# A two-block transformer kernel: earlier first matmuls, paired stick-breaking values, and another order of weight splits, taps and head copies

## The chip, the cores and the metric

One core of a Trainium2 chip. The metric is the device time of one execution in microseconds (us), the median of several runs. Matrix products run on TensorE (PE), elementwise work on VectorE (DVE), ScalarE (ACT) and GpSimd (POOL); SyncE (SP) issues most of the loads.

## What is computed

Two blocks over 512 positions of width 1024, in float32:

```python
# first block
h = rmsnorm(x, attn_norm_w); proj = h @ w_in              # 24 tiles of 128 columns
y_sb = stick_breaking_attention(q_a, k_a, v_a)            # 4 heads of 64
y_ch = chunked_relpos_attention(qh, kh, v_b, rel_bias)    # 8 heads
y_cv = short_conv_mixer(g_b, g_c, x_c, conv_w)
x = x + group_rmsnorm(concat(y_sb, y_ch, y_cv)) @ w_out
x = x + swiglu(rmsnorm(x), w_gate, w_up, w_down)
# second block
proj = rmsnorm_2(x) @ w_in_2 + b_in_2                     # 42 tiles of 128 columns
conv = silu(layernorm(causal depthwise conv, 31 taps, of val * sigmoid(gate))) @ w_conv_out
attn = sliding-window attention with sinks (16 heads, 2 kv heads, rope) @ w_attn_o
x = x + gated sum of both @ w_out_2
x = x + peer(rmsnorm_2(x))                                # 16384 experts, top 16
```

The stick-breaking weights of a head are `exp(log_sigmoid(z) + sum of log(1-beta) over nearer keys)`, and the output is these weights times v.

## The kernel before

**Layout and weights.** Activations are kept transposed: 128 channels of a tile on the partitions, the 512 positions along the free axis. Every large product is made of three fp32r matmuls per 128x128 piece of weights (`three`, L1094 to L1098): high weights times high input, high times low, low times high. So each weight slot (128x2048 elements, two output tiles of eight pieces, or k steps) is loaded into `raw`, ACT makes the rounded high part `wh` (`high`, L562 to L566) and DVE or POOL the rest `wl = raw - wh` (`weight_low`, L1708 to L1711). There are two buffers of each: ACT may write `wh` of a slot when PE has finished the slot two before it (`w_used`), PE may start a slot when its `wl` is there (`w_lo`). Inside a slot, columns 256k to 256k+255 belong to step k, 128 for each of its two output tiles. Each engine runs its own list, written out by hand, and waits on semaphores.

**The start.** SP loads x in four pairs of tiles and slot 0 in two parts, columns 0 to 511 and 512 to 2047 (L405 to L412); ACT's queue loads `vec` (all per-channel vectors, 389 columns) and later `cst`. ACT makes the high parts of x and of slot 0 (`x_high`, L569 to L572; `first_high`, L615 to L618), DVE the low ones (`x_low`, `first_low`, L1714 to L1717). PE takes the first two tiles interleaved, k step by k step (L1171 to L1177), waiting for slot 0's second part at k = 2, then tiles 2 and 3 out of slot 1, tiles 4 and 5 out of slot 2.

**Stick-breaking heads** (L1238 to L1272). For each of four heads n, PE computes four score products (`sb_scores`, L1219), nine chunks of the projection as cover (a chunk is one k step of a tile, three matmuls), the reverse sums (`sb_sums`, L1226 to L1234), five more chunks, and the values product (`sb_values`, L1238 to L1250). The scores' logs are made by ACT in the buffer `ab` (`sb_logs`, L682 to L698), softplus and masks by DVE (L1748 to L1777). All heads use one `ab`, so `sb_logs(n)` waits for the values of head n-1 (`sb_pv`). The values product has four matmuls of 512, 384, 256 and 128 columns with 64 output rows: an even head fills partitions 0 to 63 of bank 4, an odd one 64 to 127. The chunked heads that follow have a values product too (L1310), in which the matmuls of two heads alternate.

**The second block's projection** (PE L1443 to L1484, ACT L893 to L926, DVE L2080 to L2110). 42 tiles in 21 slots, g0 = FIRST["in2"], slots g0 to g0+20. Tiles 0 to 5 run on unscaled x, whose scaled high and low parts are made meanwhile (`scaled_x`, `scaled_high`); later tiles use the scaled ones. ACT evicts tile t-1 in step t (`in2_out`) and makes the high part of the slot two ahead in odd steps. DVE does the 31-tap convolution, two channel tiles alternating, one product and 31 taps each, 256 operations in all, handed out in numbers by `taps(count)`, and `weight_low`. In DVE's step t the order is: beats, `scaled_out`, for even t up to 6 `weight_low(g0+t/2+1)`, ropes, taps (5 in even, 7 in odd steps from 6 to 21), and for even t from 8 on `weight_low(g0+t/2+1)`. From tile 22 on the sliding-window attention runs between the pieces in 35 beats:

```python
def beat_place(n):
    chunk = n * (Z2_TILES - BEAT_TILE0) * KD // BEATS   # 42, 22, 8, 35
    return BEAT_TILE0 + chunk // KD, chunk % KD
```

so beats 0 to 5 stand before pieces (22,0), (22,4), (23,1), (23,5), (24,2), (24,6). PE's beat n is scores(n) (L1388), the transposes of beat n-2 (L1399), and the values of beat n-3 (L1412). scores(n) waits for DVE's `masked(n-1)` (L2065, semaphore `sw_m`), scores(0) for the first rope (`sw_q`). DVE's beat n: one tap, `masked(n)`, one tap, a rope of the next head pair if n % 4 = 1 (with one tap), two taps. ACT's beat n: for n = 7, 11, ... first `heads_out` (two copies, L863 and L869), then `turned_weights(n-2)` (L856), on which PE's values wait, then the exponentials and scales of beat n (L835 to L847).

**What the change touches:** L239 to L240 (buffers), L405 to L412, L560, L613 to L634, L688 to L710, L871 to L878, L911 to L917, L1171 to L1181, L1238 to L1272, L1666, L1714 to L1727, L1755, L1776, L2091 to L2106.

Of the kernel before, what the change touches and what calls it, by code (L numbers as in the profile page):

```python
# [15 lines left out]
P = 128  # L16
# [163 lines left out]
def build(nc, ins, out):  # L180
    with ExitStack() as ctx:
# [57 lines left out]

        csc = (z1[:, 0:2, :], z1[:, 2:4, :], ab[:, 0:2, :])  # L240
# [154 lines left out]
        def _(sp):  # L395
# [163 lines left out]
        def _(act):  # L559
            act.dma_start(vec[:, :], ins["vec"]).then_inc(sem("vec_in"), 16)  # L560
# [52 lines left out]
            act.wait_ge(sem("vec_in"), 16)  # L613

            def first_high(sem_in, part):  # L615
                c = slice(512 * part, 512 if part == 0 else 2048)
                act.wait_ge(sem(sem_in), 16)
                act.activation(wh[:, 0, c], raw[:, 0, c], ACT.Copy).then_inc(sem("w_hi" if part else "w0_hi"), 1)  # L618

            for k in range(KD):  # L620
                if k % 2 == 0:
                    act.wait_ge(sem(f"x_in{k // 2}"), 16)
                x_high(0, k)
                if k == 0:
                    first_high("w0_raw", 0)
                if k == 2:
                    first_high("w_raw0", 1)
                    act.dma_start(cst[:, :, :], ins["cst"]).then_inc(sem("cst_in"), 16)
            high(1, 1)
            for k in range(KD):  # L630
                x_square(0, k)
            high(2, 0)
            norm(0, 2)
# [48 lines left out]
            def sb_logs(n):  # L682

                for a in range(NT + 2):
                    if a < NT:
                        b, w, i = NT - 1 - a, (a + 1) * P, 4 * n + a + 1
                        act.wait_ge(sem("sb_z"), i)
                        if n:  # L688
                            act.wait_ge(sem("sb_pv"), n)
                        act.activation(ab[:, b, 0:w], ps[:, b, 0:w], ACT.Abs).then_inc(sem("sb_abs"), 1)  # L690
                    if 0 <= a - 1 < NT:
                        b, w, i = NT - a, a * P, 4 * n + a
                        act.wait_ge(sem("sb_abs"), i)
                        act.activation(ab[:, b, 0:w], ab[:, b, 0:w], ACT.Exp, scale=-1.0).then_inc(sem("sb_e"), 1)
                    if a >= 2:
                        b, w, i = NT + 1 - a, (a - 1) * P, 4 * n + a - 1
                        act.wait_ge(sem("sb_e"), i)
                        act.activation(ab[:, b, 0:w], ab[:, b, 0:w], ACT.Ln, bias=v("one")).then_inc(sem("sb_l"), 1)  # L698

            def sb_weights(n):  # L700

                for a in range(NT):
                    b, w, i = NT - 1 - a, (a + 1) * P, 4 * n + a + 1
                    act.wait_ge(sem("sb_cum"), i)
                    act.activation(ab[:, b, 0:w], ps[:, b, 0:w], ACT.Exp).then_inc(sem("sb_w0"), 1)

            def sb_out(p):

                act.wait_ge(sem("sb_pv"), 2 * p + 2)
# [191 lines left out]
            for t in range(Z2_TILES + 1):  # L901
# [9 lines left out]
                if t >= 4:  # L911
                    in2_out(t - 1)
# [1537 lines left out]
```

## Time and profile before

| | us |
|---|---|
| Runs before (3): median, lowest, highest | 2642.7, 2642.53, 2644.01 |
| The profiled execution's own time | 2642.51 |
| Its span, first to last instruction | 2640.7 |
| PE busy | 2609.4 (99%) |
| DVE busy | 1606.1 (61%) |
| ACT busy | 1042.4 (39%) |
| POOL busy | 432.6 (16%) |

The execution's time is 1.8 us more than its span. A busy PE is a PE with a matmul under way; matmul rows give start and length, and a steady stream overlaps, so its pace is read from starts. "Idle before <- X" names what ended an engine's idle time. The rows of an engine are read in order of time; L numbers are lines of the kernel before.

### The profile page before, as it was taken

To read this page: it belongs to the slowest core of one execution; us is meant where nothing else is said; L and a number is where in the kernel's file an instruction comes from. 1 tells how busy PE (TensorE), PEld (TensorE's weight loads), DVE (VectorE), ACT (ScalarE), POOL (GpSimd) and SP (SyncE) were. 2 spreads that over 40 slices of the span, in tenths; PEclk is the share of its full clock that TensorE was granted. 3 is DMA by queue.
4 is the path that set the end of the run, shared out by engine and by line. 5 is a ranking of instruction groups with operands and counts; after the bars stand their busy time and mean duration, and the time that the engine had idled before them with its cause. 6 is when DMAs were issued, how large, how long until landed. Compare 5 with 4: busy or idle time off the path is not lost.

```text
span 2640.7 us, 33826 instructions
## 1 busy us (share of the span) xinstructions
PE 2609.4 (99%) x12608; PEld 2115.0 (80%) x12608; DVE 1606.1 (61%) x2402; ACT 1042.4 (39%) x1349; POOL 432.6 (16%) x179
## 2 busy tenths in 40 slices
PE   8999999999999999999999999999999999999998
PEld 6777888888776788888888888888888888888886
DVE  4577211203999976579998988888344444444444
ACT  4565322214347763232223555555322222222223
POOL 0001455542021104434444000000000000000000
PEclk9999999999999999999999999999999999999999
DMA  5112222222222222224333454464565555555552
GB/s 185 48 51 78 96 95 95 100 96 96 96 84 76 69 96 96 106 77 145 146 147 142 171 212 183 191 238 183 214 216 192 194 195 195 195 193 195 195 191 96
DMA packets 121736, 374.37 MB, mean 142 GB/s; under 512 B 7552, under 2 KB 73216, under 8 KB 92736
## 3 DMA queue, kind: packets, MB, share of 16 engines
q1 hardware_dynamic: 117968, 333.74, 35.8%
q10 hardware_dynamic: 2016, 35.26, 3.4%
q0 software_dynamic: 1680, 4.46, 0.6%
q8 instruction: 39, 0.64, 0.1%
q14 instruction: 33, 0.27, 0.0%
HBM read 301.86 MB, written 69.21 MB: 141 GB/s over the span
## 4 chain that ended last, share of the span: by engine, by line
PE 92%; DVE 6%; ACT 1%; issue 1%; DMA 0%; POOL 0%; POOLq 0%; SPq 0%; DVEq 0%; ACTq 0%
PE ps L1096 28%; PE ps L1098 28%; PE ps L1097 28%; DVE z L2004 3%; PE ps L1619 2%; DVE wl L1711 1%; PE ps L1577 0%; PE ps L1399 0%; PE ps L1283 0%; ACT wh L566 0%; PE ps L1294 0%; PE ps L1412 0%; PE ps L1388 0%; PE ps L1310 0%; PE ps L1219 0%
## 5 line engine op out<-in xcount | busy, mean ns | idle before, releaser
L1096 PE MATMUL ps<-hh,wh 128*128 128x512 f32 x1968 | 783.9, 398 | 10.8 <-DVE wl L1717 8.5
L1098 PE MATMUL ps<-hh,wl 128*128 128x512 f32 x1968 | 769.0, 391 | 0.0
L1097 PE MATMUL ps<-hl,wh 128*128 128x512 f32 x1968 | 768.1, 390 | 0.0
L566 ACT ACTIVATE wh<-raw 128x2048 fp32r<-128x2048 f32 x217 | 414.8, 1912 | 774.3 <-PE ps L1098 772.5
L2293 DVE TENSOR_TENSOR wl<-raw,wh 128x2048 fp32r<-128x2048 f32 x101 | 231.3, 2290 | 432.1 <-ACT wh L566 432.1
L1096 PEld LDWEIGHTS ps<-hh,wh 128*128 128x128 f32 x1968 | 370.4, 188 | 101.2 <-issue 15.3
L1098 PEld LDWEIGHTS ps<-hh,wl 128*128 128x128 f32 x1968 | 370.3, 188 | 79.1
L1097 PEld LDWEIGHTS ps<-hl,wh 128*128 128x128 f32 x1968 | 370.9, 188 | 74.1 <-issue 0.7
L1097 PE MATMUL ps<-gal,wh 128*128 128x512 f32 x1024 | 398.7, 389 | 0.0
L1096 PE MATMUL ps<-gah,wh 128*128 128x512 f32 x1024 | 398.7, 389 | 0.0
L1098 PE MATMUL ps<-gah,wl 128*128 128x512 f32 x1024 | 398.7, 389 | 0.0
L478 POOL TENSOR_TENSOR wl<-raw,wh 128x2048 fp32r<-128x2048 f32 x50 | 230.4, 4608 | 588.4 <-ACT wh L566 588.4
L1097 PEld LDWEIGHTS ps<-gal,wh 128*128 128x128 f32 x1024 | 192.3, 188 | 39.8
L1096 PEld LDWEIGHTS ps<-gah,wh 128*128 128x128 f32 x1024 | 192.3, 188 | 39.8
L1098 PEld LDWEIGHTS ps<-gah,wl 128*128 128x128 f32 x1024 | 192.3, 188 | 39.8
L555 POOL TENSOR_TENSOR pf<-pf,at 128x512 f32<-128x512 f32 x3 | 3.7, 1265 | 1183.6 <-ACT at L1083 1183.6
L2004 DVE SCALAR_TENSOR_TENSOR z<-z,vec 128x511 f32<-128x511 f32 (+14 forms) x240 | 161.0, 731 | 0.0
L547 POOL TENSOR_TENSOR wl<-raw,wh 128x2048 fp32r<-128x2048 f32 x27 | 128.0, 4740 | 183.6 <-ACT wh L566 183.6
L1000 ACT ACTIVATE ast<-ps 128x512 f32<-128x512 f32 x64 | 38.2, 598 | 240.9 <-PE ps L1098 240.9
L1045 ACT ACTIVATE stage<-ps 128x512 f32<-128x512 f32 x128 | 129.4, 1122 | 0.0
L1035 ACT ACTIVATE ast<-ps 128x512 f32<-128x512 f32 x64 | 38.2, 597 | 194.8 <-PE ps L1098 194.8
L2307 DVE TENSOR_TENSOR same<-iota_t,slot_t 128x1024 f16<-128x1024 f16 x64 | 79.2, 1237 | 43.8 <-PE ps L1619 37.9
(289 smaller groups left out, 3038.6 us busy)
## 6 DMA issues: line engine op xcount, KB each, us to landing
raw<-in_w_slots SPq DMA_DIRECT2D x217, 1024.0 KB, 4.8
a_spill<-ast SPq DMA_DIRECT2D x64, 512.0 KB, 2.6
gate_table<-stage ACTq DMA_DIRECT2D x8, 4096.0 KB, 13.0
at<-a_spill SPq DMA_DIRECT2D x64, 512.0 KB, 5.7
tt<-gate_table SPq DMA_DIRECT2D x64, 512.0 KB, 6.8
lnb<-z POOLq DMA_DIRECT2D x36, 64.0 KB, 2.0
xT<-in_x SPq DMA_DIRECT2D x4, 512.0 KB, 7.3
bt<-in_rel_tiles POOLq DMA_DIRECT2D x1, 2048.0 KB, 11.9
```

Of the source, the lines that this page charges most:

```text
L478: pool.tensor_tensor(wl[:, b, :], raw[:, b, :], wh[:, b, :].bitcast(F32), ALU.subtract).then_inc(sem("w_lo"), 1)
L547: pool.tensor_tensor(wl[:, b, :], raw[:, b, :], wh[:, b, :].bitcast(F32), ALU.subtract).then_inc(sem("uv_lo"), 1)
L566: act.activation(wh[:, b, :], raw[:, b, :], ACT.Copy).then_inc(sem("w_hi"), 1)
L1000: act.activation(ast[:, 2 * b + j, :], ps[:, 4 + 2 * b + j, :], ACT.Gelu).then_inc(sem("a_ev"), 1)
L1045: act.activation(stage[:, q % 2, :, c:c + 4].rearrange("p e c -> p c e"), ps[:, 2 * j + a, :].rearrange("p (c e) -> p c e", c=4), ACT.Copy ...
L1096: nc.tensor.matmul(bank, whi, xhi, start=start, stop=False)
L1097: nc.tensor.matmul(bank, whi, xlo, start=False, stop=False)
L1098: return nc.tensor.matmul(bank, wlo, xhi, start=False, stop=stop)
L1619: last = nc.tensor.matmul(ps[:, 2 * r + t // 4, NKEYS * (t % 4):NKEYS * (t % 4) + NKEYS], oh[r][:, 0, t, :], oh[r][:, part, t, :], start=( ...
L2004: dve.scalar_tensor_tensor(acc[:, back:S], u[:, 0:S - back], w, acc[:, back:S], ALU.mult, ALU.add).then_inc(sem("cv2_y" if m == TAPS else ...
L2293: dve.tensor_tensor(wl[:, b, :], raw[:, b, :], wh[:, b, :].bitcast(F32), ALU.subtract).then_inc(sem("uv_lo"), 1)
L2307: dve.tensor_tensor(same[:, :, :], iota_rows, slots(0), ALU.is_equal).then_inc(sem("oh_part"), 1)
```

## The change

1. **Start.** x tile 0, then x tile 1 and columns 256 to 1023 of slot 0, then the rest; columns 0 to 255 of slot 0 and the first 8 columns of `vec` go over ACT's queue; slot 1 comes in two halves that wait for nothing; splits in the same parts. The rest of `vec`, and `cst`, are issued after the x splits. PE first multiplies a tile of zeros twice into bank 5.
2. **Stick-breaking values** of heads 2p and 2p+1 are computed together after head 2p+1, matmuls of the two alternating; odd heads get a buffer of their own, the last four tiles of z1, not yet in use at that time.
3. **Second block's projection.** ACT's `high(g0+4)` stands ahead of `in2_out(4)`; `weight_low(g0+5)` to `weight_low(g0+11)` stand ahead of their step's taps; `weight_low(g0+12)` stands behind beat 2, in step 23, and not behind beat 1; step 21 has 4 taps, not 7 (the three move behind the loop); ACT's `heads_out` stands at the end of its beat.

```diff
+        idle = z1[:, ORDER1[-1], :]
+        sbw = (ab, z1[:, Z1_TILES - NT:Z1_TILES, :])
...
-            x_pair(0)
-            sp.dma_start(raw[:, 0, 0:512], ins["w_slots"][0, :, 0:512]).then_inc(sem("w0_raw"), 16)
+            sp.dma_start(xT[:, 0, :], ins["x"][:, 0, :]).then_inc(sem("first_in"), 16)
+            sp.dma_start(xT[:, 1, :], ins["x"][:, 1, :]).then_inc(sem("next_in"), 16)
+            sp.dma_start(raw[:, 0, 256:1024], ins["w_slots"][0, :, 256:1024]).then_inc(sem("next_in"), 16)
             x_pair(1)
-            sp.dma_start(raw[:, 0, 512:2048], ins["w_slots"][0, :, 512:2048]).then_inc(sem("w_raw0"), 16)
+            sp.dma_start(raw[:, 0, 1024:2048], ins["w_slots"][0, :, 1024:2048]).then_inc(sem("w_raw0"), 16)
             x_pair(2)
             x_pair(3)
-            load(1, 1)
+            sp.dma_start(raw[:, 1, 0:1024], ins["w_slots"][1, :, 0:1024]).then_inc(sem("w1_raw"), 16)
+            sp.dma_start(raw[:, 1, 1024:2048], ins["w_slots"][1, :, 1024:2048]).then_inc(sem("w_raw1"), 16)
...
-            act.dma_start(vec[:, :], ins["vec"]).then_inc(sem("vec_in"), 16)
+            act.dma_start(vec[:, 0:KD], ins["vec"][:, 0:KD]).then_inc(sem("first_in"), 16)
+            act.dma_start(raw[:, 0, 0:256], ins["w_slots"][0, :, 0:256]).then_inc(sem("w0a_in"), 16)
...
             for k in range(KD):
-                if k % 2 == 0:
+                if k == 1:
+                    act.wait_ge(sem("next_in"), 2 * 16)
+                elif k and k % 2 == 0:
                     act.wait_ge(sem(f"x_in{k // 2}"), 16)
                 x_high(0, k)
                 if k == 0:
-                    first_high("w0_raw", 0)
-                if k == 2:
-                    first_high("w_raw0", 1)
-                    act.dma_start(cst[:, :, :], ins["cst"]).then_inc(sem("cst_in"), 16)
-            high(1, 1)
+                    part_high(0, 0, 256, "w0a_in", 16, "part_hi")
+                if k == 1:
+                    part_high(0, 256, 1024, "next_in", 2 * 16, "part_hi")
+                if k == 3:
+                    part_high(0, 1024, 2048, "w_raw0", 16, "w_hi")
+            act.dma_start(vec[:, KD:], ins["vec"][:, KD:]).then_inc(sem("vec_in"), 16)
+            act.dma_start(cst[:, :, :], ins["cst"]).then_inc(sem("cst_in"), 16)
+            part_high(1, 0, 1024, "w1_raw", 16, "part_hi")
+            part_high(1, 1024, 2048, "w_raw1", 16, "w_hi")
...
-                        if n:
-                            act.wait_ge(sem("sb_pv"), n)
-                        act.activation(ab[:, b, 0:w], ps[:, b, 0:w], ACT.Abs).then_inc(sem("sb_abs"), 1)
+                        if n >= 2:
+                            act.wait_ge(sem("sb_pv"), n // 2)
+                        act.activation(sbw[n % 2][:, b, 0:w], ps[:, b, 0:w], ACT.Abs).then_inc(sem("sb_abs"), 1)
...
             def beat(n):
-                if n >= 7 and (n - 7) % NT == 0:
-                    heads_out((n - 7) // NT)
                 if 0 <= n - 2 < SWA_STEPS:
                     turned_weights(n - 2)
                 if n < SWA_STEPS:
                     exps(n)
                     scaled(n)
+                if n >= 7 and (n - 7) % NT == 0:
+                    heads_out((n - 7) // NT)
...
                         scaled_high(k)
+                    high(g0 + t // 2 + 2, (g0 + t // 2) % 2)
                 if t >= 4:
                     in2_out(t - 1)
...
-                if t < Z2_TILES and t % 2:
+                if t < Z2_TILES and t % 2 and t != RAW_TILES - 1:
                     high(g0 + t // 2 + 2, (g0 + t // 2) % 2)
...
-            pe.wait_ge(sem("w0_lo"), 1)
+            pe.wait_ge(sem("idle_in"), 1)
+            for _ in range(2):
+                nc.tensor.matmul(ps[:, 5, :], idle[:, 0:P], idle, start=True, stop=True)
             for k in range(KD):
-                if k == 2:
+                if k < 2:
+                    pe.wait_ge(sem("part_lo"), k + 1)
+                if k == 4:
                     pe.wait_ge(sem("w_lo"), 3)
                 pe.wait_ge(sem("x_l"), k + 1)
                 for t in range(2):
                     in1_piece(t, k)
-            pe.wait_ge(sem("w_lo"), 1 + 3)
+            pe.wait_ge(sem("part_lo"), 3)
             for t in (2, 3):
                 for k in range(KD):
+                    if t == 2 and k == 4:
+                        pe.wait_ge(sem("w_lo"), 1 + 3)
                     in1_piece(t, k)
...
-            def sb_values(n):
-
-                p, h = n // 2, slice(HD * (n % 2), HD * (n % 2) + HD)
+            def sb_values(p):
+
...
-                pe.wait_ge(sem("sb_w"), NT * n + NT)
+                pe.wait_ge(sem("sb_w"), NT * 2 * (p + 1))
                 for b in range(NT):
-                    last = nc.tensor.matmul(ps[h, 4, b * P:S], vst[:, p, b, h], ab[:, b, 0:S - b * P],
-                                            start=(b == 0), stop=(b == NT - 1))
+                    for e in range(2):
+                        h = slice(HD * e, HD * e + HD)
+                        last = nc.tensor.matmul(ps[h, 4, b * P:S], vst[:, p, b, h], sbw[e][:, b, 0:S - b * P],
+                                                start=(b == 0), stop=(b == NT - 1))
...
-                sb_values(n)
+                if n % 2:
+                    sb_values(n // 2)
...
+            dve.memset(idle, 0.0).then_inc(sem("idle_in"), 1)
...
                 for n in beats_in(t):
                     beat(n)
+                    if n == beats_in(BEAT_TILE0 + 1)[0]:
+                        weight_low(g0 + BEAT_TILE0 // 2 + 1)
                 if t <= RAW_TILES:
                     scaled_out(t - 1)
-                if t % 2 == 0 and t <= RAW_TILES:
+                if t % 2 == 0 and t < BEAT_TILE0:
                     weight_low(g0 + t // 2 + 1)
...
                 if RAW_TILES <= t < BEAT_TILE0:
-                    taps(7 if t % 2 else 5)
-                if t % 2 == 0 and RAW_TILES < t < Z2_TILES:
+                    taps(4 if t == BEAT_TILE0 - 1 else 7 if t % 2 else 5)
+                if t % 2 == 0 and BEAT_TILE0 < t < Z2_TILES:
                     weight_low(g0 + t // 2 + 1)
```

The DVE splits of slots 0 and 1 follow ACT's parts, and softplus and masks use `sbw[n % 2]` in place of `ab`.

## Rows read from the trace of the kernel before

**Rows 1.** The page, busy time: engine, us, share of the span, instructions.
```profile
PE 2609.4 (99%) x12608; PEld 2115.0 (80%) x12608; DVE 1606.1 (61%) x2402; ACT 1042.4 (39%) x1349; POOL 432.6 (16%) x179
```
**Rows 2.** What PE waited for, whole span: us in total, times, longest.
```profile
PE ps L1388 <- DVE sstat L2065: 4.2, 3, 3.3
PE ps L1096 <- DVE wl L1711: 2.3, 2, 1.7
PE ps L1399 <- ACT sqb L856: 1.9, 2, 1.4
```
**Rows 3.** Timeline of the start: start us, length us, engine, line, operation.
```profile
5.62 0.72 ACT L572 ACTIVATE hh<-xT,vec 128x512 fp32r<-128x512 f32 x1 [3.13 <-DMA vec<-in_vec]
6.57 0.63 ACT L618 ACTIVATE wh<-raw 128x512 fp32r<-128x512 f32 x1 [0.24 <-DMA raw<-in_w_slots]
7.98 0.79 PE L1096 MATMUL ps<-hh,wh 128*128 128x512 f32 x1 [7.98 <-DVE wl L1717]
9.75 1.48 ACT L618 ACTIVATE wh<-raw 128x1536 fp32r<-128x1536 f32 x1 [1.19 <-DMA raw<-in_w_slots]
10.71 0.63 PE L1096 MATMUL ps<-hh,wh 128*128 128x512 f32 x1
11.27 1.76 DVE L1717 TENSOR_TENSOR wl<-raw,wh 128x1536 fp32r<-128x1536 f32 x1 [1.93 <-ACT wh L618]
13.08 0.50 PE L1096 MATMUL ps<-hh,wh 128*128 128x512 f32 x1 [0.53 <-DVE wl L1717]
```
**Rows 4.** The chain that ended last, 95 to 240 us: start, us, what.
```profile
97.95 2.30 PE ps L1248 x8
...
156.49 1.02 PE ps L1310 x16
```
**Rows 5.** Timeline of DVE and PE in and behind the last stick-breaking head.
```profile
107.73 0.29 DVE L1760 TENSOR_TENSOR yT<-yT,cst 128x128 f32<-128x128 f32 x1
...
111.23 1.02 PE L1226 MATMUL ps<-yT,cst 128*128 128x512 f32 x2
...
123.47 0.70 PE L1283 MATMUL ps<-z 64*128 64x256 f32 x4 [0.30 <-DVE z L1836]
```
**Rows 6.** Timeline of PE in the second block's projection.
```profile
679.90 0.39 PE L1096 MATMUL ps<-hh,wh 128*128 128x512 f32 x1
...
687.15 0.39 PE L1098 MATMUL ps<-hh,wl 128*128 128x512 f32 x1
...
770.75 0.70 PE L1388 MATMUL ps<-kdup,z 64*128 64x256 f32 x4 [3.31 <-DVE sstat L2065]
...
772.82 0.63 PE L1097 MATMUL ps<-hl,wh 128*128 128x512 f32 x1
```
**Rows 7.** Stretch of PE alone: stretch, us, PE busy (x), PEclk, DMA share, GB/s.
```profile
770.70:777.50 6.80, 6.75 (x27) 0.75 0.36 142
```
**Rows 8.** Timeline of DVE in the second block's projection.
```profile
674.00 2.29 DVE L1711 TENSOR_TENSOR wl<-raw,wh 128x2048 fp32r<-128x2048 f32 x1 [2.00 <-ACT wh L566]
...
678.32 8.65 DVE L2004 SCALAR_TENSOR_TENSOR z<-z,vec 128x511 f32<-128x511 f32 x13
686.88 2.29 DVE L1711 TENSOR_TENSOR wl<-raw,wh 128x2048 fp32r<-128x2048 f32 x1
...
758.55 0.35 DVE L2065 CUSTOM_DVE_ANT_0 tmp_all<-ps,msk,nsink 128x128 f32<-128x128 f32 x1
...
766.87 2.28 DVE L1711 TENSOR_TENSOR wl<-raw,wh 128x2048 fp32r<-128x2048 f32 x1
...
778.80 0.35 DVE L2065 CUSTOM_DVE_ANT_0 tmp_all<-ps,msk,nsink 128x128 f32<-128x128 f32 x1 [2.27 <-PE ps L1399]
...
802.53 2.28 DVE L1711 TENSOR_TENSOR wl<-raw,wh 128x2048 fp32r<-128x2048 f32 x1
```
**Rows 9.** Timeline of ACT in the same stage.
```profile
795.54 1.91 ACT L566 ACTIVATE wh<-raw 128x2048 fp32r<-128x2048 f32 x1
...
798.50 0.58 ACT L856 ACTIVATE sqb<-ps 128x512 f32<-128x512 f32 x1
```

More of the change, by code:

```diff
@@ L612, in _, with part_high @@
             ln_exp_tables()
[L613 to L618, printed above, removed]
+            act.wait_ge(sem("first_in"), 2 * 16)
+            def part_high(b, c0, c1, loaded, count, done):
+                act.wait_ge(sem(loaded), count)
+                act.activation(wh[:, b, c0:c1], raw[:, b, c0:c1], ACT.Copy).then_inc(sem(done), 1)
             for k in range(KD):
-                if k % 2 == 0:
+                if k == 1:
+                    act.wait_ge(sem("next_in"), 2 * 16)
+                elif k and k % 2 == 0:
                     act.wait_ge(sem(f"x_in{k // 2}"), 16)
@@ L693, in sb_logs @@
                         act.wait_ge(sem("sb_abs"), i)
-                        act.activation(ab[:, b, 0:w], ab[:, b, 0:w], ACT.Exp, scale=-1.0).then_inc(sem("sb_e"), 1)
+                        act.activation(sbw[n % 2][:, b, 0:w], sbw[n % 2][:, b, 0:w], ACT.Exp, scale=-1.0).then_inc(sem("sb_e"), 1)
                     if a >= 2:
@@ L697, in sb_logs @@
                         act.wait_ge(sem("sb_e"), i)
-                        act.activation(ab[:, b, 0:w], ab[:, b, 0:w], ACT.Ln, bias=v("one")).then_inc(sem("sb_l"), 1)
+                        act.activation(sbw[n % 2][:, b, 0:w], sbw[n % 2][:, b, 0:w], ACT.Ln, bias=v("one")
+                                       ).then_inc(sem("sb_l"), 1)
             def sb_weights(n):
@@ L704, in sb_weights @@
                     act.wait_ge(sem("sb_cum"), i)
-                    act.activation(ab[:, b, 0:w], ps[:, b, 0:w], ACT.Exp).then_inc(sem("sb_w0"), 1)
+                    act.activation(sbw[n % 2][:, b, 0:w], ps[:, b, 0:w], ACT.Exp).then_inc(sem("sb_w0"), 1)
             def sb_out(p):
-                act.wait_ge(sem("sb_pv"), 2 * p + 2)
+                act.wait_ge(sem("sb_pv"), p + 1)
                 act.activation(yT[:, p, :], ps[:, 4, :], ACT.Copy).then_inc(sem("sb_y"), 1)
@@ L1712, in weight_low, with part_low @@
                                   ).then_inc(sem("w_lo"), 1)
-            def first_low(half):
-                c = slice(512 * half, 512 if half == 0 else 2048)
-                dve.wait_ge(sem("w_hi" if half else "w0_hi"), 1)
-                dve.tensor_tensor(wl[:, 0, c], raw[:, 0, c], wh[:, 0, c].bitcast(F32), ALU.subtract
-                                  ).then_inc(sem("w_lo" if half else "w0_lo"), 1)
+            def part_low(b, c0, c1, high_done, count, done):
+                dve.wait_ge(sem(high_done), count)
+                dve.tensor_tensor(wl[:, b, c0:c1], raw[:, b, c0:c1], wh[:, b, c0:c1].bitcast(F32), ALU.subtract
+                                  ).then_inc(sem(done), 1)
             dve.sem_inc(sem("x_tile"), 8)
@@ L1723, in _ @@
                 if k == 0:
-                    first_low(0)
-                if k == 2:
-                    first_low(1)
-            weight_low(1)
+                    part_low(0, 0, 256, "part_hi", 1, "part_lo")
+                if k == 1:
+                    part_low(0, 256, 1024, "part_hi", 2, "part_lo")
+                if k == 3:
+                    part_low(0, 1024, 2048, "w_hi", 1, "w_lo")
+            part_low(1, 0, 1024, "part_hi", 3, "part_lo")
+            part_low(1, 1024, 2048, "w_hi", 2, "w_lo")
             for k in range(KD):
@@ L1775, in masked @@
                     dve.wait_ge(sem("sb_w0"), NT * n + a + 1)
-                    dve.scalar_tensor_tensor(ab[:, b, 0:P], ab[:, b, 0:P], 3.0e38, upper, ALU.min, ALU.mult
-                                             ).then_inc(sem("sb_w"), 1)
+                    own = sbw[n % 2][:, b, 0:P]
+                    dve.scalar_tensor_tensor(own, own, 3.0e38, upper, ALU.min, ALU.mult).then_inc(sem("sb_w"), 1)
             def head_normed(z):
```

9 lines of the change are left out of this document (5 added, 4 removed).

## The prediction, made before the kernel was run

> **What bounds the kernel now.** I read the page first: PE is busy in 99% of the span [rows 1], so a change pays by what it takes off PE's own list or out of PE's pauses. Hence the list of PE's waits [rows 2]: before scores (L1388) 4.2 us, before projection pieces for DVE's `wl` 2.3 us, before values (L1399, for ACT's L856) 1.9 us; all these stand in the second block's projection. Next the start's timeline [rows 3], where PE has nothing until 7.98. Then what PE itself spends on values products [rows 4], the slack behind them [rows 5], and PE, DVE and ACT in the second projection [rows 6 to 9]. PE's full pace is one 128x512 matmul in 0.227 us: 32 starts from 679.90 to 687.15 [rows 6]. A piece (three) is 0.68 us, a slot of 48 is 10.9 us.
>
> **1. The start: 2.4 us gained.** Before, PE's stream is unbroken from 13.08 on with 12 matmuls done; at full pace that equals a start at 13.08 - 12 x 0.227 = 10.36.
> Loads: by 5.62 there had landed x pair 0 (512 KB) and `vec` (194.5 KB); by 6.57 another 256 KB, together 962 KB; by 9.75 pair 1 and 768 KB more, 2242 KB [rows 3]. So 402 KB/us between the last two, 269 between the first two. The first piece now needs 256 KB of x, 4 KB of `vec` and 128 KB of weights: 318 KB less than had landed at 5.62, that is 0.8 to 1.2 us earlier; I take 4.7. Columns 256 to 1023 and x tile 1 end at 1028 KB: 6.57 + 66 / 402 = 6.7.
> Splits: ACT's copy takes 0.63 for 512 columns and 1.48 for 1536, so 0.42, 0.84, 1.05 for 256, 768, 1024; DVE's subtraction 1.76 for 1536 [rows 3] and 2.29 for 2048 [rows 8], so 0.43, 0.96, 1.23. First piece: x high 4.7 to 5.4, copy to 5.9; DVE x low to 6.2 (0.70, 512 columns by the same rows), part low to 6.65. PE at 6.7, six matmuls, done at 8.1. Second: x high 6.8 to 7.5, copy to 8.35, DVE low to 9.35. PE goes on at 9.35 with six done: equal to a start at 8.0. Against 10.36: **2.4**. Columns 1024 on end at 2052 KB, 9.3; their low part is ready at about 11.9, PE asks at 9.35 + 18 x 0.227 = 13.4. Slot 1's first half ends at 3588 KB, 13.1, low at about 16; PE asks at 8.0 + 10.9 = 18.9. Both are covered by 1.5 us or more; gone, they would cost their excess one for one. The rest of `vec`, and `cst`, are moved behind eight x copies on ACT's queue; they are first needed at the mean square, 21.8 us behind the start, and cost nothing.
> The zero product: DVE's memset, PE's two float32 products with twice 512 x 4 columns' passes. L1248 shows 1280 columns in 2.30 us at full pace [rows 4], so two of 512 at half pace take 3.7; from about 1.7 they end near 5.4, before 6.7. It costs nothing. What it is for shows in the rows: the matmuls from 7.98 to 10.71 last 0.63 where later ones last 0.39 [rows 3, 6], 1.2 against 2.4 GHz. Since PE still waits for the second part until 9.35, warm matmuls only count from there.
> Bounds: 0.9 (next parts land 0.7 late as well as a clock at 1.2 GHz for half of its stretch) to 3.2.
>
> **2. Paired values: 4.6 us gained.** Before there are four products of 2.30 [rows 4] = 9.2. In the chunked heads, matmuls of two heads alternate between the two halves of output partitions: 8 matmuls of 128 columns, 1024 columns, take 1.02 [rows 4], 1.00 ns a column, where L1248, one head alone, takes 2.30 / 1280 = 1.80 ns. So a pair of 2560 columns takes 2.3 to 2.56. The short one carries more of fixed cost, so I take 2.3: 9.2 - 4.6 = **4.6**. Bounds: 0 (no overlap at 512 columns) to 4.7.
> Who gets late when PE arrives 2.3 us earlier behind head 0 and again behind head 2? Head 3 is the tight one: ACT is occupied before its logs, so its chain stays where it is while PE moves up. The last softplus mask ends at 107.73 + 0.29 = 108.0; PE's sum that needs it moves from 111.23 to 108.9 [rows 5]. Covered by 0.9. Behind it PE waits 0.30 at 123.47 [rows 5] for a chain that begins with PE's own last head norm in head 3's tail; both ends move together, so the 0.30 stays. The freed wait (`sb_logs(1)` and `(3)` for values) gives nothing by itself, PE never waited there.
>
> **3. The second projection: 7.3 us gained.** I keep the times of before.
> (a) DVE's split at 674.00 had waited 2.00 for ACT's copy [rows 8], which now stands ahead of `in2_out(4)`. DVE is free at 672.0, so low g0+4 is ready 1.9 us earlier, PE's pause before it (2.3 - 1.7 = 0.6 [rows 2]) goes.
> (b) The next split, 686.88 [rows 8], moves ahead of five taps. A tap is 8.65 / 13 = 0.665 [rows 8]: 3.3 us, plus 1.9 from (a), against a pause of 1.7 [rows 2]. It goes. With two pipeline refills, (a) + (b) = **2.5**. After that each slot leaves DVE 12 taps (8.0) and a split (2.2) = 10.2 against PE's 10.9, so the splits stay ahead; each waits for ACT's copy, which follows PE by 2.2, and is then needed 8.7 later.
> (c) The beats. `masked(0)` at 758.55 [rows 8] moves up by the three taps that go (2.0) and part of the 1.9, less what DVE now waits for ACT's copies on the way (about 1.2) and with the split's gain: I get 756.4, its end at 757.0. PE, now due at 752.7, first waits about 0.5 for the rope, then 0.6 for this mask: scores(1) at 757.0, before 759.33 (4.2 - 3.3 = 0.9 in two waits, one of them 0.7). Then DVE has 4 taps, `masked(1)`, a rope with its tap (3.1), 2 + 1 taps, and no split: `masked(2)` runs 765.4 to 766.2, where before it stood behind the split of 766.87 to 769.15 [rows 8]. PE, due at 765.1, goes on at 766.3 and not at 770.75: a pause of 1.1 in place of 3.31 [rows 6]. Then two taps and low g0+12 to 770.4; PE asks for it at 770.0, 0.4 lost. That is the wait that takes the old one's place.
> Behind the 3.31 the granted clock was 0.75 over 6.8 us [rows 7], the lower level for half of that, matmuls lasting 0.63 again [rows 6]: 6.8 x 0.25 = 1.7 us lost. Pauses of 1.7 in this stage drew no such row [rows 2], so at 1.1 it stays at 2.4 GHz. Sum: old 4.0 (0.7 + 3.3) + 1.7, new 0.5 + 0.6 + 1.1 + 0.4 = 2.6; **3.1** gained. DVE can follow: it waited 2.27 for PE at 778.80 [rows 8]. The three deferred taps (2.0 us) run behind the loop, ahead of a layer-norm sum that PE takes only three tiles (16 us) into the next product.
> (d) `heads_out` stood between the copy that ends at 797.45 and `turned_weights` at 798.50 [rows 9], whose start is thus some 1.15 later than need be (two copies that overlap the neighbours by 0.1). PE's two pauses there are 1.4 and 1.9 - 1.4 = 0.5 [rows 2]: 1.15 + 0.5 = **1.7**. In return `in2_out` and `high` stand behind two copies when a head pair ends; the copy ready at 797.45 is taken by DVE at 802.53 [rows 8], 5.1 in hand. Cost nothing.
> Bounds of 3: 4.0 (a, b, d without c, less small change) to 9.5 (nothing waits).
>
> **Sum.** 2.4 + 4.6 + 2.5 + 3.1 + 1.7 = 14.3. The profiled execution took 2642.5 (span 2640.7), the median is 2642.7, 0.2 apart; 2642.5 - 14.3 = **2628.2**. About 0.2% (5.3 us) is what a measurement can tell from no change.
>
> The Trainium skill (TensorE: Matmul & The Clock Gate, part 1) says that the array's default state is the throttled one and that activity releases it; by that page the zero product releases the clock, and the pauses around the first piece may close it again, which is rival B. This case's trace agrees as far as the half pace behind 3.31 us goes.
>
> **Rivals.**
> A, the sum above: 2628.2, 0.5.
> B, the clock falls back in the start. PE idles 5.4 to 6.7 and 8.1 to 9.35, much like the 3.31 that was followed by slow matmuls; against it, pauses of 1.7 were not. Price 1.7 as at 772.3 [rows 7]: 2629.9, 0.17.
> C, DVE stays late in the beats: if its list reaches beat 2 2 us later than I sum, the pause and the slow clock remain, (c) gives 0: 2631.3, 0.14.
> D, the pair does not overlap at 512 columns: + 4.6, 2632.8. For it: the only overlapping rows are 128 columns long. 0.08.
> E, the change doesn't do what it says: gains in front are given back at some later wait for a load or an engine. Against it: in the rest of the kernel PE's waits sum to a few us. Within 0.2%, 0.05.
> F, slower: ACT. If `heads_out` at the beat's end makes `high` so late that DVE's split misses its slot, each of six head pairs costs PE a pause like 3.3 and a slow stretch of 1.7: 30 us, against 14.3: 2658. It decides only beyond 5.1 us of delay [rows 8, 9], the move gives 1.15. 0.02. Another 0.04 lies faster than A's own range.
>
> **The numbers.** Faster by over 0.2%: 0.93; within: 0.05; slower: 0.02. Range: A's own bounds reach from 2625 to 2631; with B, C and most of D, 2624.8 to 2633.0.
>
> **What would show it.** Right: first real matmul near 6.7, unbroken from near 9.4; two rows of x16 at L1248's successor with 2.3 to 2.6 each; no wait for `wl` before slots g0+4 and g0+5; waits before scores(1) and scores(3) near 0.6 and 1.1, one of 0.4 before slot g0+12, and granted clock 1.00 around them; ACT's L856 before the head copies. Wrong: pairs of 4.6; a clock row of 0.75 in that stage; a new PE wait on `wl` in the beats of more than 1 us; an unbroken start later than 10.

## The result, and the profile after

The changed kernel takes 2629.1 us (median of five runs, 2628.5 to 2630.2) against 2642.7 us before (2642.4 to 2644.0): ratio 0.9948, 95% interval 0.9937 to 0.9959. That is 13.6 us less; I had said 14.3 less and 2628.2 us. The profiled execution took 2629.1 with a span of 2627.3, 13.4 below the span of before.

The page of the changed kernel, busy time; it answers to [rows 1]:
```profile
PE 2606.8 (99%) x12612; PEld 2112.3 (80%) x12612; DVE 1606.7 (61%) x2405; ACT 1042.3 (40%) x1351; POOL 422.4 (16%) x179
```
PE's busy time fell by 2.6 us although 3.8 us of zero products came in; its idle time (span less busy) fell from 31.3 to 20.5. So busy time alone tells little of this change. What PE waited for, whole span (us in total, times, longest), as in [rows 2]:
```profile
PE ps L1410 <- DVE sstat L2091: 1.7, 3, 1.1
PE ps L1110 <- DVE wl L1740: 1.4, 1, 1.4
PE ps L1421 <- ACT sqb L869: 1.0, 2, 0.7
PE ps L1410 <- DVE z L2080: 0.5, 1, 0.5
```
PE's waits for the masks fell from 4.2 to 1.7; the two for `wl` in the second projection are gone from this list (the 1.4 left is the start's); those of the transposes for ACT's copy fell from 1.9 to 1.0. The way to read the difference is to follow one matmul of PE through both traces and note by how much it starts earlier. L numbers in a row are lines of the kernel that the row is from: in the changed kernel L1110 to L1112 are the three matmuls of a piece, L1269 the stick-breaking values, L1410 the scores, L1421 the transposes; `...` stands for rows left out. Timeline of PE, changed kernel:
```profile
1.47 3.78 PE L1187 MATMUL ps<-z 128*128 128x512 f32 x4 [1.47 <-DVE z L1689]
6.62 0.80 PE L1110 MATMUL ps<-hh,wh 128*128 128x512 f32 x1 [1.37 <-DVE wl L1740]
7.21 0.63 PE L1111 MATMUL ps<-hl,wh 128*128 128x512 f32 x1
...
9.37 0.80 PE L1110 MATMUL ps<-hh,wh 128*128 128x512 f32 x1
...
10.39 0.40 PE L1112 MATMUL ps<-hh,wl 128*128 128x512 f32 x1
...
30.37 1.02 PE L1117 MATMUL ps<-lnb,cst 128*128 128x512 f32 x2
...
74.86 0.64 PE L1269 MATMUL ps<-ab,vst 128*64 128x512 f32 x1
...
77.17 2.42 PE L1239 MATMUL ps<-z 64*128 64x128 f32 x8
...
104.75 0.59 PE L1246 MATMUL ps<-yT,cst 128*128 128x512 f32 x1
...
116.98 0.70 PE L1305 MATMUL ps<-z 64*128 64x256 f32 x4 [0.28 <-DVE z L1862]
...
746.34 0.49 PE L1410 MATMUL ps<-kdup,z 64*128 64x128 f32 x4 [0.53 <-DVE z L2080]
...
750.13 0.70 PE L1410 MATMUL ps<-kdup,z 64*128 64x256 f32 x4 [0.35 <-DVE sstat L2091]
...
759.36 0.70 PE L1410 MATMUL ps<-kdup,z 64*128 64x256 f32 x4 [1.14 <-DVE sstat L2091]
...
763.40 0.50 PE L1110 MATMUL ps<-hh,wh 128*128 128x512 f32 x1
...
764.98 0.49 PE L1410 MATMUL ps<-kdup,z 64*128 64x128 f32 x4
...
785.63 0.63 PE L1421 MATMUL ps<-cst,tmp_all 128*128 128x128 f32 x4 [0.26 <-ACT sqb L869]
...
830.17 0.70 PE L1410 MATMUL ps<-kdup,z 64*128 64x256 f32 x4 [0.18 <-DVE sstat L2091]
...
891.57 0.63 PE L1421 MATMUL ps<-cst,tmp_all 128*128 128x128 f32 x4 [0.72 <-ACT sqb L869]
```
The same matmuls in the kernel before, where they are not in the rows ahead of the prediction:
```profile
32.28 1.02 PE L1103 MATMUL ps<-lnb,cst 128*128 128x512 f32 x2
...
777.57 0.49 PE L1388 MATMUL ps<-kdup,z 64*128 64x128 f32 x4
...
844.31 0.70 PE L1388 MATMUL ps<-kdup,z 64*128 64x256 f32 x4 [0.17 <-DVE sstat L2065]
...
904.92 0.66 PE L1399 MATMUL ps<-cst,tmp_all 128*128 128x128 f32 x4
```
| PE matmul | before | after | earlier by | so this part |
|---|---|---|---|---|
| mean square | 32.28 | 30.37 | 1.91 | start 1.91 (forecast 2.4) |
| head normalisation behind head 3 | 123.47 [rows 5] | 116.98 | 6.49 | values 4.58 (4.6) |
| scores(3), with the pause behind `masked(2)` | 770.75 [rows 6] | 759.36 | 11.39 | |
| scores(4) | 777.57 | 764.98 | 12.59 | 3 (a) to (c) 6.10 (5.6) |
| the next scores with a pause | 844.31 | 830.17 | 14.14 | 3 (d) 1.55 (1.7) |
| transposes near the stage's end | 904.92 | 891.57 | 13.35 | a new pause, -0.79 (0) |
| the span | 2640.7 | 2627.3 | 13.4 | |

At 830 the kernel is 14.1 ahead, nearly the forecast; 0.8 is given back at one place and nothing moves behind it. ACT's timeline there, changed kernel:
```profile
889.04 1.90 ACT L571 ACTIVATE wh<-raw 128x2048 fp32r<-128x2048 f32 x1
890.85 0.58 ACT L869 ACTIVATE sqb<-ps 128x512 f32<-128x512 f32 x1
```
The second row is `turned_weights`' copy, which empties the bank that PE's transposes at 891.57 write. Ahead of it stand `heads_out` (two copies from 887.32 on), `in2_out` (888.47) and `high`, the weight copy of 1.90: `heads_out` now ends its beat, and where the beat ends a step, the other two follow before the next beat begins. The wait is that of the transposes (L1399 before), not that of the values, as the prediction has it.

One wait is too short for the list. PE's matmul at 763.40 is the first of slot g0+12, and DVE's split for that slot ends just ahead of it (DVE, changed kernel):
```profile
761.04 2.30 DVE L1734 TENSOR_TENSOR wl<-raw,wh 128x2048 fp32r<-128x2048 f32 x1
```
From scores(3) to scores(4), five pieces apart, the changed kernel takes 764.98 - 759.36 = 5.62. In e10 below, where this split is ready in time, it takes 5.25:
```profile
756.96 0.70 PE L1412 MATMUL ps<-kdup,z 64*128 64x256 f32 x4
...
762.21 0.49 PE L1412 MATMUL ps<-kdup,z 64*128 64x128 f32 x4
```
So the wait for slot g0+12 costs 0.37, and the same five pieces in the kernel before, 777.57 - 770.75 = 6.82, lost 1.57 to the slow clock.

In the beats of the changed kernel the granted clock stayed whole, against 0.75 in [rows 7] (stretch, us, PE busy, PEclk, DMA share, GB/s):
```profile
757.70:764.50 6.80, 5.55 (x29) 1.00 0.21 42
```

### The profile page after: what moved, and what is told of

Its sections match the earlier page's. It is cut to its first block, busy times and chain, and to the rows that moved or that the text cites. A ratio compares the mean times of both kernels' runs of the same rounds, so it can differ in the third digit from the quotient of the medians.

```text
span 2627.3 us, 33837 instructions
## 1 busy us (share of the span) xinstructions
PE 2606.8 (99%) x12612; PEld 2112.3 (80%) x12612; DVE 1606.7 (61%) x2405; ACT 1042.3 (40%) x1351; POOL 422.4 (16%) x179
## 4 chain that ended last, share of the span: by engine, by line
PE 95%; DVE 3%; ACT 1%; issue 1%; DMA 0%; POOL 0%; POOLq 0%; ACTq 0%; DVEq 0%
PE ps L1110 30%; PE ps L1112 29%; PE ps L1111 29%; PE ps L1641 2%; DVE z L2030 1%; DVE wl L1734 1%; PE ps L1599 0%; PE ps L1305 0%; PE ps L1421 0%; PE ps L1316 0%; PE ps L1434 0%; PE ps L1332 0%; PE ps L1410 0%; ACT wh L571 0%; PE ps L1239 0%
## 5 line engine op out<-in xcount | busy, mean ns | idle before, releaser
L1110 PE MATMUL ps<-hh,wh 128*128 128x512 f32 x1968 | 782.6, 398 | 1.5 <-DVE wl L1740 1.4
L1112 PE MATMUL ps<-hh,wl 128*128 128x512 f32 x1968 | 767.8, 390 | 0.0
L1110 PEld LDWEIGHTS ps<-hh,wh 128*128 128x128 f32 x1968 | 369.8, 188 | 92.5 <-issue 15.3
L1112 PEld LDWEIGHTS ps<-hh,wl 128*128 128x128 f32 x1968 | 369.8, 188 | 79.6
L1110 PE MATMUL ps<-gah,wh 128*128 128x512 f32 x1024 | 398.3, 389 | 0.0
L1112 PE MATMUL ps<-gah,wl 128*128 128x512 f32 x1024 | 398.3, 389 | 0.0
L1110 PEld LDWEIGHTS ps<-gah,wh 128*128 128x128 f32 x1024 | 192.3, 188 | 39.9
L1112 PEld LDWEIGHTS ps<-gah,wl 128*128 128x128 f32 x1024 | 192.3, 188 | 39.9
```

The source lines that it names most:

```text
L1110: nc.tensor.matmul(bank, whi, xhi, start=start, stop=False)
L1112: return nc.tensor.matmul(bank, wlo, xhi, start=False, stop=stop)
```

## The experiments

Each run is a change to the changed kernel, executed and profiled once unless more is said; the kernel before took 2642.7 in the same sets of runs, and 2643.2 beside the last two. Single executions differ in the start and, by up to 0.9 (e1), in the output's last transfers, so I read each run by the shift of PE's matmuls against the changed kernel: at the mean square (30.37, the start alone), behind the second projection (935.39), and the difference of the two.

| run | time | mean square | behind projection | difference |
|---|---|---|---|---|
| e1_no_zero | 2631.2 | +1.2 | +1.2 | 0.0 |
| e2_zero_three | 2628.7 | -0.4 | -0.4 | 0.0 |
| e3_heads_first | 2630.1 | 0.0 | +0.9 | +0.9 |
| e4_heads_split | 2628.2 | -0.2 | -0.9 | -0.7 |
| e5_values_by_head | 2632.1 | +0.1 | +2.9 | +2.8 |
| e6_split12_taps_back | 2634.3 | -0.2 | +5.1 | +5.4 |
| e7_taps_back | 2632.0 | +0.7 | +2.9 | +2.2 |
| e8_all_three | 2625.8 | 0.0 | -3.4 | -3.4 |
| e9_after_again | 2629.1 (5 runs) | -0.6 | -0.6 | +0.1 |
| e10_all_three_timed | 2625.5 (5 runs) | -0.2 | -3.7 | -3.5 |

Behind the projection no run shifts again until the last matmul: what is gained or lost up to 935 is what the span shows, but for the output's last transfers.

**e1_no_zero and e2_zero_three: the zero products.** e1 takes them out, with their memset; e2 adds a third:
```diff
-            for _ in range(2):
+            for _ in range(3):
                 nc.tensor.matmul(ps[:, 5, :], idle[:, 0:P], idle, start=True, stop=True)
```


> The changed kernel without the two zero products and their memset; all else as changed. In the changed kernel the matmuls from 6.62 us on last 0.63 us and are 0.43 apart until about 10.2, although the zero products ran from 1.47 to 5.25. Theory Z (the zero products do nothing, because a pause of 1.4 us stands behind them): full pace begins at 9.8 to 10.6 as with them, the mean square's matmul starts at 30.37 plus or minus 0.4, and the span stays at 2627.3 plus or minus 0.5. Theory W (they bring the full pace forward part of the way): without them the full pace begins 3.2 us or more behind 6.62 and up to 1 us later than with them, and the span grows by 0.2 to 0.7.

> The changed kernel with three zero products in place of two, so that PE is at work without a pause until the first real piece. Theory P (it was the pause that kept the clock low): the first real matmuls are 0.23 apart, the second group still starts at about 9.4 because its weights are not there, full pace equals a start at 8.1 in place of 8.6, the mean square comes 0.5 earlier, the span is 0.5 shorter. Theory N (zero operands release nothing, or not that soon): slow matmuls as before until 10 or later, the first piece some 0.3 to 0.5 later, span the same or up to 0.4 longer.

PE's timeline without them:
```profile
7.40 0.79 PE L1110 MATMUL ps<-hh,wh 128*128 128x512 f32 x1 [7.40 <-DVE wl L1736]
...
12.26 0.43 PE L1112 MATMUL ps<-hh,wl 128*128 128x512 f32 x1
```
and with three:
```profile
1.47 5.49 PE L1187 MATMUL ps<-z 128*128 128x512 f32 x6 [1.47 <-DVE z L1689]
6.66 0.79 PE L1110 MATMUL ps<-hh,wh 128*128 128x512 f32 x1
...
7.54 0.40 PE L1112 MATMUL ps<-hh,wl 128*128 128x512 f32 x1
...
9.38 0.50 PE L1110 MATMUL ps<-hh,wh 128*128 128x512 f32 x1 [0.76 <-DVE wl L1740]
```
Without them matmuls start 0.43 apart (1.2 GHz) until 12.26; in the changed kernel until 10.39; with three, from 7.54 on none does. But then PE is done with the first piece early and waits 0.76 for the second, whose low part is ready at the same 9.3: of the faster pace only 0.4 is left. e2 thus came out nearly as theory P has it in its numbers (0.4 for 0.5). Its cause, that it was the pause that kept the clock low, is not shown: e8 and e10, with three products too, had a pause of 0.39 and 1.05 ahead of the first piece and ran it at full pace.

Neither theory for e1 held: the mean square came 1.2 later, more than either allowed. Of this, 0.8 is a first piece that was itself 0.8 later (7.40), and that is the load of its weights: ACT's copy of them begins at 6.47, against 5.69 in the changed kernel, and it was as late in e7 (6.42), which has the zero products. So 0.4 is left for the two products; single executions whose starts differ by as much do not fix it further.

**e3_heads_first and e4_heads_split: the head copies.** e3 puts `heads_out` back to the beat's front; e4 does so only for the two that end a step:
```diff
             def beat(n):
+                if n in (27, 31):
+                    heads_out((n - 7) // NT)
...
-                if n >= 7 and (n - 7) % NT == 0:
+                if n >= 7 and (n - 7) % NT == 0 and n not in (27, 31):
                     heads_out((n - 7) // NT)
```


> The changed kernel with the head copies back at the beginning of ACT's beat, and nothing else undone. My theory: the pauses of 0.26 and 0 at the first two head pairs grow back to 1.4 and about 0.5 us, and the new pause of 0.72 at 891.57 goes: net 0.8 slower, span 2628.1. Rival (that new pause comes from the earlier PE and not from the place of the copies): it stays, the span is 2628.9.

> The changed kernel with the head copies at the end of the beat, except in beats 27 and 31, the last beats of an odd step, where they stand at the beginning; there a copy of a whole slot follows them on ACT ahead of the next turned weights. My theory: the pause of 0.72 at 891.57 goes and none comes in its place, span 0.8 shorter, 2626.5. Rival (the slot's copy is late anyway): the pause stays, span 2627.3.

PE's waits for the copies (us, times, longest) in e3; in e4 a single one of 0.3 is left:
```profile
PE ps L1421 <- ACT sqb L869: 1.9, 2, 1.4
```
With the copies in front both old pauses are back and the new one is gone: + 0.9, which is 1.67 given up less 0.72 to 0.8 won. With only the two moved, the old pauses stay away and the new one goes: - 0.7, its size. This shows that the pause at 891.57 is the price of the order inside the beat, and that it is not needed.

**e5_values_by_head: the paired values.**
```diff
-                for b in range(NT):
-                    for e in range(2):
+                for e in range(2):
+                    for b in range(NT):
```


> Edit: in the paired values product the four matmuls of the first head stand ahead of the four of the second; nothing else. Theory (my prediction's: the pair costs what one head costs because matmuls that alternate between the two halves of the output partitions overlap, two by two): here only the last matmul of the first head and the first of the second can overlap, by at most 128 columns' time (0.06 us), so a pair takes 2.3 + 2.2 = 4.5 us where the changed kernel's rows have 2.31, both together + 4.4: span 2631.7, time 2633.5, and everything ahead of the first pair is unchanged. Rival (PE lets a matmul begin as soon as its own half is free, whatever the order: in the chunked heads four matmuls in the order first, first, second, second took 0.59 us, no longer than the alternating ones): a pair stays between 2.3 and 2.8 and the span within 1 us of 2627.3.

PE's timeline in e5; rows with `ab` are of the first head, rows with `z` of the second, and each matmul of the kernel shows as two in the rows:
```profile
76.49 0.64 PE L1269 MATMUL ps<-z,vst 128*64 128x512 f32 x1
76.70 0.49 PE L1269 MATMUL ps<-ab,vst 128*64 128x256 f32 x2
...
77.03 0.27 PE L1269 MATMUL ps<-ab,vst 128*64 128x128 f32 x1
77.40 1.46 PE L1269 MATMUL ps<-z,vst 128*64 128x384 f32 x6
78.79 2.42 PE L1239 MATMUL ps<-z 64*128 64x128 f32 x8
```
Neither expectation held. The first head begins at 74.93 and PE's next work at 78.79, so a pair takes 3.9 where the changed kernel's takes 2.3: 1.6 more, not 2.2 and not 0. The rows show why it is less than two heads in a row: the second head's first matmul starts at 76.49, while three rows of the first head are still to start (two from 76.70 on, one at 77.03). So, by the starts in the profile, PE does begin a matmul of the free half ahead of queued ones of the busy half, but only over the last few, and in alternation the overlap is whole. (The rival's four matmuls of 0.59 us do not speak for it: in the kernel's code those of the chunked heads' values product alternate too.) Behind the second pair the shift falls from 3.2 to 2.9, since the pause of 0.28 at 116.98 takes it up.

**e6_split12_taps_back and e7_taps_back: the beats.** e7 puts back the three taps ahead of them, e6 also the split for slot g0+12 (the edit of e6; e7 has its taps line alone):
```diff
-                    if n == beats_in(BEAT_TILE0 + 1)[0]:
-                        weight_low(g0 + BEAT_TILE0 // 2 + 1)
...
-                    taps(4 if t == BEAT_TILE0 - 1 else 7 if t % 2 else 5)
-                if t % 2 == 0 and BEAT_TILE0 < t < Z2_TILES:
+                    taps(7 if t % 2 else 5)
+                if t % 2 == 0 and BEAT_TILE0 <= t < Z2_TILES:
```


> Edit: DVE's split for the slot after the next (low part of g0+12) goes back ahead of the beats' third tile, as before the change, and the tile ahead of the beats has its seven taps again instead of four; all else stays as changed. Theory (part c of my prediction: the split and three taps ahead of the third mask were the cause of the pause of 3.31 us and of the slow clock behind it): PE's pause in front of the third and fourth scores (1.14 in the changed kernel, at 759.4) comes back at about 1.1 + 2.2 (split) = 3.3 or more, up to 3.3 + 2.0 with the taps; the first mask's wait grows by up to 2.0; and in the 7 us behind the pause there is a stretch with a granted clock below 1.00 and matmuls of 0.63. Span + 3.3 to + 6 (2630.6 to 2633.3). Rival (the slow clock of before was no result of that pause): the pause comes back, matmuls behind it stay at full pace, and the span grows by the pauses alone.

> Edit: only the three taps go back to the tile ahead of the beats (seven instead of four); the split for g0+12 stays where the change put it. Theory: DVE is what PE waits for before the first mask and the third (0.35 and 1.14 us in the changed kernel), and three taps are 3 x 0.665 = 2.0 us of its time, so both together grow by 2.0: the span is 2629.3, and more by up to 1.7 if the longer pause is followed by slow matmuls. Rival (DVE waits there for PE or ACT, and takes the taps into that idle time): both pauses unchanged within 0.3, span within 0.5 of 2627.3.

PE in the beats of e6, then PE's stretch behind the long pause:
```profile
763.31 0.70 PE L1410 MATMUL ps<-kdup,z 64*128 64x256 f32 x4 [3.29 <-DVE sstat L2091]
```
```profile
763.30:770.10 6.80, 6.79 (x29) 0.75 0.35 141
```
and PE in the beats of e7, the first mask and the third:
```profile
752.83 0.70 PE L1410 MATMUL ps<-kdup,z 64*128 64x256 f32 x4 [2.29 <-DVE sstat L2091]
...
762.05 0.70 PE L1410 MATMUL ps<-kdup,z 64*128 64x256 f32 x4 [1.09 <-DVE sstat L2091]
```
e6 brings back the pause of [rows 6] to 0.02 us and the 0.75 of [rows 7] with it. The taps cost 1.94 at the first mask (2.29, in both, against 0.35), three times 0.65; the second pause does not grow by them, since PE comes 1.94 later to it too. The split's place, in which alone e6 differs from e7, costs 2.20 (3.29 against 1.09). From scores(3) to scores(4) e6 takes 770.06 - 763.31 = 6.75, with no wait for slot g0+12: 1.50 more than the 5.25 of e10, and that is the slow clock. By these terms e6 is 2.20 + 1.50 - 0.37 = 3.3 behind e7; the table has 3.2. The rival that the slow clock had another cause is refuted as far as this goes: behind 1.09 and 2.29 of pause the rows show a granted clock of 1.00, behind 3.29 one of 0.75. That it depends on the pause alone, whatever stands around it, no run here shows.

**e8_all_three, and the last two, timed.** Three zero products, e4's two head copies (edit above), and five more taps moved behind the loop:
```diff
-            for _ in range(2):
+            for _ in range(3):
...
-                    taps(4 if t == BEAT_TILE0 - 1 else 7 if t % 2 else 5)
+                    taps({BEAT_TILE0 - 1: 0, BEAT_TILE0 - 2: 4}.get(t, 7 if t % 2 else 5))
```


> Edits, on the changed kernel: three zero products instead of two; the head copies of the two head pairs that end with a step stand ahead of the beat's other work instead of behind it; and of DVE's taps ahead of the beats one more goes from the tile before the last and four from the last (4 and 0 instead of 5 and 4), to behind the loop. Theory: - 0.4 for the zero product, - 0.9 for the head copies, as each had alone, and DVE is 5 x 0.665 = 3.3 us earlier at the first mask, so the waits of 0.53 (rope), 0.35 (first mask) and 1.14 (third mask) go as far as nothing but DVE sets them: - 1.0 to - 2.0. Sum - 2.3 to - 3.3: span 2624.0 to 2625.0. Rival 1: the rope and masks wait for PE's and ACT's own results by then, so only the first two terms come: 2626.0. Rival 2: the eight taps that now stand behind the loop (5.3 us) make the layer-norm sum late, which had 3.5 us in hand with three of them; the five more cost 3.3, so up to 0.2 is lost there, or more if DVE's other work moved too.

> The changed kernel as it is, timed beside the next one on the same chip, for a direct comparison. Expected 2629.1 (2628.5 to 2630.3), as measured before: 13.5 less than the kernel before. Its start should again have the first piece near 6.7, matmuls at half pace until about 10 to 11 and a mean square between 30.1 and 31.1, as the spread of the looks so far (30.1 to 31.1 in five executions with two zero products).

> Three zero products, the two head copies of a step's end ahead, eight taps behind the loop: the version of the look at 2625.8, timed. If that look was typical: 2625.8 within 0.8, faster than the changed kernel by 2.5 to 3.8, since 2.1 us of it are pauses of PE for DVE's masks and rope (0.53 + 0.35 + 1.14), 0.9 to 1.2 the head copies, and 0 to 0.4 the zero product. If the look was a lucky one and the zero product decides (spread of the start's loads 0.8 us), the difference shrinks to about 2.0 and its interval reaches below 1.5.

PE's waits for masks and rope, 2.2 us in four waits in the changed kernel, are a single one of 0.2 in e10. The pauses of 0.53, 0.35 and 1.14 are gone, and with them the 0.26 at 785.63 and the 0.37 for slot g0+12. With e4's 0.7 that is 3.4, against 3.4 (e8) and 3.5 (e10) in the table. e8's sum, at most 3.3, was met with other terms: the zero product, booked at 0.4, gave nothing (its mean square comes at the changed kernel's time), and the five taps gave 2.7 and not 1.0 to 2.0. Timed on one chip beside each other in five runs each, e9 takes 2629.1 (2628.5 to 2629.5) and e10 2625.5 (2625.2 to 2626.2); against the kernel before, 0.9948 (0.9934 to 0.9961) and 0.9934 (0.9921 to 0.9948). So e10 beats both kernels: 3.6 us faster than the changed one, with ranges that do not touch. In their two profiled executions the third zero product has no part in it: e9's mean square came 0.4 before e10's, since e9's start, against its expectation, was at full pace throughout. Rival 2 came close: DVE ends the eight taps and the sums behind them just in time (DVE, then PE, in e10),
```profile
928.37 3.07 DVE L2043 TENSOR_TENSOR z<-z 128x512 f32<-128x512 f32 x4
...
931.65 1.02 PE L1532 MATMUL ps<-z,cst 128*128 128x512 f32 x2
```
ready at 931.4, wanted at 931.65. By that one tap more (0.65) would have made a pause.

## Why the prediction was right, and where it was off

The time, 2629.1, is 0.9 from 2628.2 and inside A's own range, and each named part gave its gain. That the sum came as near as 0.9 is in part luck: it had 0.5 too much for the start and nothing for a new pause of 0.8, and 0.4 too little for (a) and (b). By its steps:

**1. The start, 2.4 forecast, 1.91 in the profiled execution.** The times summed from loads and splits came: first real matmul at 6.62 (forecast 6.7), second part taken at 9.37 (9.35). The first came by another path: x was there 0.4 earlier than taken (4.27, not 4.7), and what set the start was the load of the first weights, for which ACT waited until 5.69. The step that failed is "PE goes on at 9.35 with six done: equal to a start at 8.0", which took full pace from there. Full pace began at 10.39 with eight done: 10.39 - 8 x 0.227 = 8.57. The zero products did not raise the clock before their pause of 1.37, and the first piece ran at 1.2 GHz; it had room for that, the two matmuls behind 9.37 had not. Rival B had the place right; but the clock had not fallen back, it had not risen, and the price was 0.5, not 1.7. In e9, the same kernel, it had risen:
```profile
1.47 3.44 PE L1187 MATMUL ps<-z 128*128 128x512 f32 x4 [1.47 <-DVE z L1689]
6.34 0.50 PE L1110 MATMUL ps<-hh,wh 128*128 128x512 f32 x1 [1.43 <-DVE wl L1740]
```
the zero products end 0.34 sooner, everything behind is at full pace, and the start is worth 1.91 + 0.63 = 2.5. So 2.4 and 1.9 are both this kernel's.

**2. The values, 4.6 forecast, 4.58.** A pair takes 2.31 (74.86 to 77.17), what one head alone took. Head 3's tight place had 0.9 in hand as said: the last mask ends at 103.83 and PE's sum starts at 104.75 (DVE's row, changed kernel).
```profile
103.55 0.28 DVE L1786 TENSOR_TENSOR yT<-yT,cst 128x128 f32<-128x128 f32 x1
```
The pause of 0.30 stayed (0.28). The Trainium skill (TensorEngine Tiling (Array Packing), Key Properties) says that different tiles of the array can execute in parallel. The trace agrees, and e5 shows that here it depends on the order of issue: without alternation the pair takes 3.9. Rival D is refuted.

**3. (a) and (b), 2.5; (c), 3.1.** Together 5.6 forecast, 6.10 measured. The pauses forecast as 0.5, 0.6, 1.1 and 0.4 are 0.53, 0.35, 1.14 and, for slot g0+12, 0.37. The slow clock cost 1.57, where 1.7 was taken from 6.8 x 0.25. So (c) is 0.70 - 0.53 - 0.35 + 3.31 - 1.14 - 0.37 + 1.57 = 3.19: right in its steps too, with two misses of 0.2 and 0.1 that go against each other. (a) and (b) are the remaining 2.9, 0.4 more than taken: both waits for `wl` are gone, and each cost more than its row says. Before, PE's starts around the second, at 687.15 [rows 6] and 689.23, are 2.08 apart, 1.85 more than the pace, and the start behind that one comes 0.1 late too: 1.96 for a wait listed as 1.69 (in the same way 0.90 for 0.64). The term that was too small is the "two pipeline refills": 0.27 each, not 0.1.
```profile
689.23 0.50 PE L1096 MATMUL ps<-hh,wh 128*128 128x512 f32 x1 [1.69 <-DVE wl L1711]
```
The layer-norm sum behind the three deferred taps was not late: DVE ended at 931.9, PE asked at 935.39. Rival C (DVE late in the beats) is refuted, and e6 shows what it would have cost.

**4. (d), 1.7 forecast, 1.55; and the "Cost nothing" behind it failed.** The pauses 1.40 and 0.53 became 0.26 and none. But I had asked only who waits for `high` (DVE, 5.1 in hand) and not who waits for the next beat's own copy behind `in2_out` and `high`. Two beats with head copies, 27 and 31, end an odd step, in which `high` follows. Behind beat 27 ACT came 0.72 late; behind beat 31 the same order just held (ACT's copy ends at 909.8, PE's transposes start at 910.05). That is the term of 0.8 missing from the sum, and e4 takes it back. Rival F had the engine and the order right, but not the waiting instruction.

Measured: 1.91 + 4.58 + 6.10 + 1.55 - 0.79 = 13.35, the span's 13.4. No run takes back the start's loads or (a) and (b) alone; for these, the waits that are gone and the shift of PE's matmuls are the evidence.

## What to carry to other kernels

When an operation moves to the end of an iteration, follow everything queued up to the next iteration's first result on that engine, at every kind of boundary (here, beats that also end a step), not only the consumer of the item that is delayed. Parts of an engine's list that are needed much later, such as the taps, are worth moving out of a stretch in which that engine is behind, as far as their own deadline allows; in this case eight taps, 5.3 us, with 0.2 left. A wait in the profile's list can cost more than its length and a short one can be missing from it (0.37 here): the distance between starts, against the same piece of work without the wait, shows both. Where two products write different halves of the output partitions, issue them in alternation: one behind the other they overlapped only at the seam here (3.9 us against 2.3).

## What the runs showed of the hardware that I had not expected

The start's clock differs between executions of the same code. Of seven executions with two zero products, five ran the first piece at half pace, as above, one at full pace throughout (e9), and one as follows (PE in e7, timeline, then two stretches with PEclk ahead of the DMA share):
```profile
1.47 3.55 PE L1187 MATMUL ps<-z 128*128 128x512 f32 x4 [1.47 <-DVE z L1689]
7.35 0.50 PE L1110 MATMUL ps<-hh,wh 128*128 128x512 f32 x1 [2.33 <-DVE wl L1740]
...
8.20 0.63 PE L1110 MATMUL ps<-hh,wh 128*128 128x512 f32 x1
```
```profile
6.60:9.30 2.70, 1.95 (x6) 0.77 1.02 412
9.30:12.00 2.70, 2.70 (x8) 0.60 1.02 384
```
The clock had risen within the zero products (3.55 us where others took 3.78), held over a pause of 2.33 into the first piece, and then fell to 1.2 GHz in the middle of work. The mean square started anywhere from 29.7 to 31.1 in these seven, in part because loads landed at different times. In the three with three zero products (e2, e8, e10) it started from 30.0 to 30.4, all at full pace from the third matmul of the first piece on. In e8 and e10 the products ended sooner than in e2 (4.79 and 4.38 us against 5.49), so there the clock had risen within them, and it held over the pauses of 0.39 and 1.05. What these ten executions have in common is thus not the pause: where the clock had risen by the end of the zero products the first piece began at full pace, and where it had not the piece began at half pace. Whether three products always suffice, three executions do not show. The Trainium skill (TensorE: Matmul & The Clock Gate, part 1) says that how many matmuls run slow at a start varies from run to run; the trace agrees: with two zero products it was none (e9) to nine (e3) from the first piece on.

In the changed kernel's start, matmuls of 0.63 stand in a stretch whose PEclk is given as 1.00 (6.60 to 9.30), and so they do in the kernel before (7.90 to 10.90), while behind a fall the column shows it (0.77, 0.60 above). So in these starts the length of the matmuls tells the clock, not the column.
